# A two-block transformer kernel: latent heads scored in pairs, and the HGRN block's RMS root moved behind its projections

## The reference, cut to what matters

```python
x = layer_norm(DN_ALPHA * x + gate * y, ln_g[layer, 1], ln_b[layer, 1])   # the last line of the first block

def rmsnorm(x, gain):
    y = xf * lax.rsqrt(jnp.mean(xf * xf, axis=-1, keepdims=True) + EPS)
    return (y * gain).astype(x.dtype)

h = h + hgrn2_mixer(rmsnorm(h, hgrn_norm[l]), w_q, w_f, w_i, w_g, ...)
    q = silu(xn @ w_q);  forget = lb + (1 - lb) * sigmoid(xn @ w_f)
    v = xn @ w_i;        gate = silu(xn @ w_g)
```

```python
s = einsum('bqhd,bkhd->bhqk', qn, k_nope) + einsum('bqhr,bkr->bhqk', qr, k_rope)
s = where(k_pos <= q_pos, s * scale, -inf);  p = softmax(s);  o = einsum('bhqk,bkhv->bqhv', p, v)
```

## Time and profile before

| | |
|---|---|
| median of 3 runs | 1435.94 us (1432.33 to 1441.17) |
| the profiled execution | 1434.05 us, its span 1432.3 us |
| TensorE busy | 1340.0 us, 94% of the span |
| VectorE busy | 1006.3 us, 70% |
| ScalarE busy | 593.3 us, 41% |
| chain that ended last | TensorE 80%, VectorE 10%, DMA 4%, ScalarE 3%, issue 2% |
| mean granted clock of TensorE | 0.967 |

### The profile page before, as it was taken

The page is one execution under the profiler, slowest core; times in us unless marked ns, Lnnn a source line. Parts: engine busy times, 40 slices in busy tenths (PEclk is TensorE's granted clock), DMA queues, the critical chain, the costliest instruction groups (busy, mean ns, idle before and its releaser), DMA issues.

```text
span 1432.3 us, 20744 instructions
## 1 busy us (share of the span) xinstructions
PE 1340.0 (94%) x7946; PEld 1127.5 (79%) x7946; DVE 1006.3 (70%) x1345; ACT 593.3 (41%) x796; POOL 13.3 (1%) x23
## 2 busy tenths in 40 slices
PE   5986989999999989999979989999999999999997
PEld 1763678888798878888869987888888777888886
DVE  2767488988878778867776785766668565566665
ACT  2443443434344543343354323543437543543432
POOL 0000000000000000000000000000000000000000
PEclk7997989999999989999989999999999999999999
DMA  9753428878377436656535330555553330455540
GB/s 381 285 199 118 165 101 323 332 268 307 122 261 243 148 118 250 249 209 220 187 120 198 118 118 30 207 193 188 180 201 118 118 118 30 162 210 201 194 158 30
DMA packets 45791, 264.18 MB, mean 184 GB/s; under 512 B 5399, under 2 KB 7063, under 8 KB 19994
## 3 DMA queue, kind: packets, MB, share of 16 engines
q1 hardware_dynamic: 32624, 218.19, 41.8%
q10 hardware_dynamic: 13102, 45.09, 9.1%
HBM read 260.89 MB, written 1.05 MB: 183 GB/s over the span
## 4 chain that ended last, share of the span: by engine, by line
PE 80%; DVE 10%; DMA 4%; ACT 3%; issue 2%; SPq 0%; POOL 0%; DVEq 0%; ACTq 0%; POOLq 0%
PE banks L555 16%; PE banks L557 15%; PE banks L556 15%; PE banks L878 14%; PE banks L881 7%; DMA A<-ada_w 2%; PE banks L834 2%; PE banks L1177 2%; DVE w_lo L1781 2%; PE banks L774 1%; DMA raw<-stream 1%; PE banks L721 1%; ACT w_hi L1219 1%; PE banks L756 1%; PE banks L787 1%
## 5 line engine op out<-in xcount | busy, mean ns | idle before, releaser
L1781 DVE TENSOR_TENSOR w_lo<-raw,w_hi 128x2048 fp32r<-128x2048 f32 x193 | 439.5, 2287 | 122.0 <-ACT w_hi L1219 119.8
L1219 ACT ACTIVATE w_hi<-raw 128x2048 fp32r<-128x2048 f32 x193 | 368.3, 1914 | 226.7 <-PE banks L557 199.5
L878 PE MATMUL banks<-hT,w_hi 128*128 128x512 f32 x896 | 280.8, 395 | 0.0
L555 PE MATMUL banks<-w_hi,R 128*128 128x512 f32 (+1 forms) x624 | 245.0, 393 | 6.4 <-DVE R L1761 3.4
L556 PE MATMUL banks<-w_lo,R 128*128 128x512 f32 (+1 forms) x624 | 242.0, 388 | 0.0
L557 PE MATMUL banks<-w_hi,R 128*128 128x512 f32 (+1 forms) x624 | 242.0, 388 | 0.0
L881 PEld LDWEIGHTS banks<-hT,w_lo 128*128 128x128 f32 x896 | 168.3, 188 | 39.2
L881 PE MATMUL banks<-hT,w_lo 128*128 128x256 f32 x896 | 176.0, 278 | 0.0
L555 PE MATMUL banks<-hT,w_hi 128*128 128x256 f32 x536 | 159.1, 297 | 7.9 <-DVE hT L2240 5.6
L556 PE MATMUL banks<-hT,w_hi 128*128 128x256 f32 x536 | 154.6, 288 | 0.0
L557 PE MATMUL banks<-hT,w_lo 128*128 128x256 f32 x536 | 154.5, 288 | 0.0
(11 more groups left out here) (254 smaller groups left out, 1515.9 us busy)
## 6 DMA issues: line engine op xcount, KB each, us to landing
raw<-stream SPq DMA_DIRECT2D x193, 1024.0 KB, 4.8
A<-ada_w ACTq DMA_DIRECT2D x73, 512.0 KB, 5.5
A<-ada_w SPq DMA_DIRECT2D x6, 1024.0 KB, 16.7
raw<-ada_w SPq DMA_DIRECT2D x3, 1024.0 KB, 7.4
A<-ln_g ACTq DMA_DIRECT2D x4, 512.0 KB, 3.8
A<-ln_b ACTq DMA_DIRECT2D x4, 512.0 KB, 5.6
...
```

The costliest lines, as they stand in the source:

```text
L555: pe.matmul(o, lh, rh, start=start, stop=False, skip_group_check=True)
L878: pe.matmul(two(B[2 * kp + a]), wh[:, kt, P * a:P * a + P], hT[:, :, kt, :], start=kt == 0, stop=False, skip_group_check=True)
L1219: act.activation(w_hi[:, s, :], raw[:, s, :], ACT.Copy).then_inc(hi_done, 1)
L1781: v.tensor_tensor(w_lo[:, s, :], raw[:, s, :], w_hi[:, s, :], ALU.subtract).then_inc(lo_done, 1)
```

## The change

Two edits are joined. At the seam, `hT` is now made from the layer norm's result before its own gain: the columns `sc_c` and `bi_c` hold the layer norm's gain and bias, each times the RMS gain, so `hT` is the input of the projections but for one factor per token, the RMS root. That factor is worked out afterwards from the squares (GpSimd's `root(2, 2, ...)`), and is applied to the projections' results: by ScalarE as the scale of its read for value and gate fills (half the root in `nw` for the gate), and for query and forget fills, whose tokens lie along the row, by a multiplication on VectorE with a row that TensorE spreads over the partitions (`token_spread`) and ScalarE copies out of bank 2 (`token_row`). The two led value fills go to banks 4 and 5. `hg_start` stands behind the two value fills, and VectorE's finishing of a query or forget fill is a step of its own, `bend`, behind the next `rest`.

In latent attention `qk_pair(k)` scores heads k and k+1 at every even step: first the four 128-row products, then the four 64-row products, the two heads' in turn (head k's rows are partitions 0 to 63, head k+1's are 64 to 127), then one mask matmul per head over both blocks. The pairs take banks 4, 5 and 2, 3 in turn, VectorE takes both heads' maxima at the even step, and the transposes behind steps 11 to 17 use banks 0 and 1.

```diff
+        def fill_bank(u, i):
+            return {HG: 4, HG + 1: 5}.get(u, i % 2)
...
-            value = lambda u, j: fills(u, "N", "h", "plain", [arena(H_V, TT, D)[:, :, 256 * j:256 * j + 256]])
-            s = [("hg_start",)] + value(HG, 0) + rest(HG + 4) + value(HG + 1, 1) + rest(HG + 5)
+            value = lambda u, j: fills(u, "N", "h", "value", [arena(H_V, TT, D)[:, :, 256 * j:256 * j + 256]])
+            s = value(HG, 0) + rest(HG + 4) + value(HG + 1, 1) + [("hg_start",), ("token_row",)]
             for j in range(4):
-                s += fills(HG + 2 + j, "T", "h", "silu", [A[:, H_Q + 512 * j:H_Q + 512 * (j + 1)]]) + rest(HG + 6 + j)
+                f = fills(HG + 2 + j, "T", "h", "silu", [A[:, H_Q + 512 * j:H_Q + 512 * (j + 1)]])
+                s += f + rest(HG + 5 + j) + [("bend",) + f[0][1:]]
                 if j == 1:
                     s += [("clear",)]
             for j in range(4):
-                s += fills(HG + 6 + j, "T", "h", "forget", [j]) + rest(HG + 10 + j)
+                f = fills(HG + 6 + j, "T", "h", "forget", [j])
+                s += f + rest(HG + 9 + j) + [("bend",) + f[0][1:]]
+            s += rest(HG + 13)
...
-        STEPS += bound(3, "lnrms", M1 + 31, own("hgrn"), lead=(HG, HG + 1)) + hg_steps()
+        STEPS += bound(3, "lnrms", M1 + 31, mod, lead=(HG, HG + 1)) + hg_steps()
...
+                if reader in ("silu", "forget"):
+                    n["z"] += 1
+                    held[b] = (z_done, n["z"])
+                if u == HG + 2:
+                    pe.wait_ge(token_root, 1)
+                    claim(2)
+                    pe.matmul(B[2][:, 0:256], ones[:, :], A[:, H_DIAG:H_DIAG + 256], start=True, stop=True).then_inc(token_spread, 1)
+                    held[2] = (token_row, 1)
...
-            def qk(k):
-                h, bank = head(k), B[4 + k % 2]
-                all_of(h["units"])
-                if k >= 2:
-                    pe.wait_ge(exp_done, k - 1)
+            def qk_pair(k):
+                heads = [head(k), head(k + 1)]
+                at = 4 if k % 4 == 0 else 2
+                for h in heads:
+                    all_of(h["units"])
+                if at == 2:
+                    for b in (2, 3):
+                        claim(b)
+                        held[b] = (exp_done, k + b - 1)
+                elif k >= 4:
+                    pe.wait_ge(exp_done, k - 2)
+                part = lambda e, t: B[at + e][:, 0:128] if t == 0 else B[at + e][:, 128:384]
+                for e in range(2):
+                    for t in range(TT):
+                        q, kk, _, _ = heads[e]["qk"][0]
+                        pe.matmul(part(e, t), q[:, P * t:P * t + P], kk[:, 0:P * (t + 1)], start=t == 0, stop=False,
+                                  skip_group_check=True)
                 for t in range(TT):
-                    o = bank[:, 0:128] if t == 0 else bank[:, 128:384]
-                    for i, (q, kk, off, w) in enumerate(h["qk"]):
-                        pe.matmul(o, q[off:off + w, P * t:P * t + P], kk[off:off + w, 0:P * (t + 1)], start=i == 0,
+                    for e in range(2):
+                        q, kk, off, w = heads[e]["qk"][1]
+                        pe.matmul(part(e, t), q[off:off + w, P * t:P * t + P], kk[off:off + w, 0:P * (t + 1)], start=False,
                                   stop=False, skip_group_check=True)
-                    m = pe.matmul(bank[:, 256 * t:256 * t + P], ident_b[:, :], causal_b[:, :], start=False, stop=True,
-                                  skip_group_check=True)
-                m.then_inc(s_done, 1)
+                for e in range(2):
+                    pe.matmul(B[at + e].rearrange("p (a b) -> p a b", b=256)[:, :, 0:P], ident_b[:, :],
+                              causal_b[:, :].unsqueeze(1).to_broadcast([P, 2, P]), start=False, stop=True,
+                              skip_group_check=True).then_inc(s_done, 1)
...
-                        if reader == "silu":
-                            act.activation(dst, bank[:, :], ACT.Copy, scale=0.5)
-                        elif reader == "gate":
-                            act.activation(dst, two(bank[:, :]), ACT.Copy, scale=0.5)
-                        act.activation(e, bank[:, :], ACT.Tanh, scale=0.5).then_inc(e_done, 1)
+                        if reader == "gate":
+                            for t in range(TT):
+                                y = bank[:, 256 * t:256 * t + 256]
+                                act.activation(dst[:, t, :], y, ACT.Identity, scale=nw[:, 0, t:t + 1], bias=zero8[:, 0:1])
+                                ins = act.activation(e[:, 256 * t:256 * t + 256], y, ACT.Tanh, scale=nw[:, 0, t:t + 1])
+                        else:
+                            act.wait_ge(z_done, n["e"] + 1)
+                            ins = act.activation(e, dst if reader == "silu" else e, ACT.Tanh)
+                        ins.then_inc(e_done, 1)
...
                     if what == "lnrms":
                         normalise(0, False)
-                        square(0)
-                        normalise(0, True)
-                        normalise(1, False)
+                        act.wait_ge(col_ready, b + 2)
                         turned(0, 0, *scales)
                         turned(1, 1, *scales)
-                        square(1)
                         ahead(last_unit - 1)
-                        normalise(1, True)
+                        normalise(1, False)
                         n["pair"] += 1
                         turned(3, 3, *scales)
                         ahead(last_unit)
+                        square(0)
+                        square(1)
...
+                elif kind == "token_row":
+                    act.wait_ge(token_spread, 1)
+                    act.activation(A[:, H_SCALE:H_SCALE + 256], B[2][:, 0:256], ACT.Copy).then_inc(token_row, 1)
...
+                    if reader in ("silu", "forget"):
+                        z = dst if reader == "silu" else A[:, H_E + 512 * (n["z"] % 2):][:, 0:512]
+                        n["z"] += 1
+                        v.wait_ge(unit_done, u + 1)
+                        v.wait_ge(token_row, 1)
+                        v.tensor_tensor(two(z), two(B[fill_bank(u, n["fill"])][:, :]),
+                                        A[:, H_SCALE:H_SCALE + 256].unsqueeze(1).to_broadcast([P, 2, SEQ]), ALU.mult).then_inc(z_done, 1)
+                    n["fill"] += 1
+                    if reader == "gate":
+                        bend(reader, dst)
...
                     if what == "lnrms":
+                        g_c, b_c = (vec[:, COL[c] + 3 * KT:COL[c] + 4 * KT] for c in ("ln_g", "ln_b"))
+                        gain = vec[:, COL["hgrn"]:COL["hgrn"] + KT]
+                        mark(v.tensor_tensor(sc_c[:, :], g_c, gain, ALU.mult))
+                        v.tensor_tensor(bi_c[:, :], b_c, gain, ALU.mult).then_inc(col_ready, 1)
                         residual(0)
                         row_root(0, False)
-                        residual(1, (0,))
+                        residual(1)
+                        split_part(0, 0)
+                        row_variance(1, False)
+                        split_part(0, 1)
+                        row_shift(1)
+                        half(False)
                         normalised()
                         affine(0)
-                        residual(1, (1,))
-                        square_root(0)
-                        row_root(1, False)
-                        half(False)
+                        stage()
+                        low(last_unit + SLOTS - 1, (last_unit - 1) % SLOTS)
                         v.wait_ge(half_ready, n["half"])
-                        n["n"] += 1
                         normalised()
                         affine(1)
-                        split_tile(0, hT_hi, hT_lo)
-                        square_root(1)
-                        half(True)
-                        stage()
+                        low(last_unit + SLOTS, last_unit % SLOTS)
+                        for t in range(TT):
+                            n["sq"] += 1
+                            v.wait_ge(sq_done, n["sq"])
+                        link(v.tensor_tensor(ve[:, 2:4], ss[:, :, 0], ss[:, :, 1], ALU.add))
+                        v.tensor_scalar(ve[:, 2:4], ve[:, 2:4], 1.0 / D, RMS_EPS, ALU.mult, ALU.add).then_inc(var_ready, 1)
+                        root_made()
+                        link(v.tensor_scalar(nw[:, 0, 0:2], rstd[:, 2:4], 0.5, None, ALU.mult))
+                        for t in range(TT):
+                            ins = v.tensor_scalar(A[:, H_DIAG + P * t:][:, 0:P], ident[:, :], nw[:, 0, t:t + 1], None, ALU.mult)
+                        ins.then_inc(token_root, 1)
+                        continue
```

116 lines of the change are left out of this document (65 added, 51 removed).

## The result

| | before | joined |
|---|---|---|
| median | 1435.60 us (1432.33 to 1441.17, 4 runs) | 1421.38 us (1420.31 to 1425.12, 4 runs) |
| ratio of the two, 95% interval | | 0.9895 (0.9865 to 0.9924) |
| profiled execution, its span | 1434.05, 1432.3 | 1425.12, 1423.3 |
| TensorE busy | 1340.0 | 1327.8 |
| VectorE busy | 1006.3 | 1009.4 |

The change saves 14.2 us, 10.9 to 19.4 by the interval. The forecast was 1425, 10.5 less than the median of before; the measured time lies in its range, though not in the 1423 to 1427 of its likeliest case. The profiled execution of the joined kernel took 1425.12, the slowest of its four; that this equals the forecast is chance, since it lost its time where nothing was changed: MLP 1's last product ends 3.96 us later than in the profile of before (719.77 for 715.81). In later executions of these kernels that moment lay anywhere from 711.6 to 721.0.

The account below looks back on a forecast made before the run. TensorE, under way for 94% of the span, was taken as the bound. Seam and front 2.8 plus heads 7.7 gave 10.5 us off the median of 1435.94, so 1425 us, range 1417 to 1433.

Parts of the forecast that it names:

- likeliest case: Whole kernel: the forecast itself, 1423 to 1427 us, chance 0.46.
- The seam, what goes: Behind MLP 1: second normalisation, ScalarE's second pass and gain multiplication leave the path; first fill at 719.9, 8.2 us earlier.
- The path to the root: VectorE's work after the first fill up to the RMS root and diagonal blocks: root there at 738.0.
- The stand in front of HG+4: TensorE waits 3.2 us from 746.0, as the level table lands at 745.5; the clock's fall costs 1.9 more.
- no second stand: Rival at the seam: table lands before VectorE is free, or clock stays up; 1420 to 1423 us, chance 0.20.
- The multiplications at nothing: Query and forget fills: eight VectorE multiplications, 5.5 us, cost nothing else, covered by that engine's waits for ScalarE.
- the gate reads at 0.45: Gate fills: four ScalarE instructions of 256 columns for two of 512 cost 0.45 us, once, at the last gate slab.
- Seam and front together: From MLP 1's end through the fills: 2.8 us gained, from -1 to +8.
- The heads: Latent attention with paired scores: 5.9 with fills, 1.0 without, 0.8 at the end; 7.7 us gained, from 4 to 10.
- a pair without fills: Later latent heads: the pair takes 5.9 us where two heads took 6.16, held by the copy that empties bank 6.
- the rule of the Trainium skill: Tiling speeds up TensorE, not PSUM's emptying; by it alone heads with fills gain no more than without, 3 us in all.
- The sum: Whole kernel: 2.8 + 7.7 = 10.5 us off, 1425 us against the median of before.

Follow-up runs that it names:

- table_late: Joined kernel with ScalarE's queue waiting for the second high part (HG+5's) before it issues the level table's load; 1432.41 us, ratio to before 0.9970.
- z_narrow: Joined kernel with the multiplications by the row of roots taking 2 of every 256 columns, same places and waits; 1421.79 us, ratio to before 0.9886.
- gate_whole: Joined kernel with each gate fill read by two ScalarE instructions of 512 columns instead of four of 256; 1421.66 us, ratio to before 0.9893.
- joined_again: The joined kernel unchanged, run once more beside two later kernels; 1421.80 us, ratio to before 0.9899.

## Why the prediction was right, and where it was not

- **The seam, what goes: right.** First fill 8.2 us earlier, measured 8.17; in the frame of before 719.91, forecast 719.9. The clock was low behind it and cost 1.7 for the 1.6 taken.
- **The path to the root: right within 0.6.** VectorE's diagonal blocks end at 741.37, in the frame of before 737.41; forecast 738.0.
- **The stand in front of HG+4: wrong, and the likeliest case with it.** I forecast 3.2 us of waiting and 1.9 for the clock, and got 0.30 and none. The step that failed is "ScalarE, which waits for it, reads HG, makes a high part and reads HG+1, and can issue the table's load while the next high part runs: 742.0". It had the wrong thing hold the load back: the work listed ahead of it, where it was the waits listed ahead of it. In that frame the load went out at 737.89, 4.1 earlier. Its own semaphore had been there for 9.2 us; ScalarE's queue stood at the first read's wait for the root, and once that had ended (741.40) it issued the load within 0.45 us, with the first of the six instructions running and five not begun. The load took 4.9 us to land and not 3.5, which ate 1.4 of the 4.1, and the multiplication ended at 746.23 instead of 749.2. table_late forces the load behind the work, as I had taken it, and gives the stand (6.40) and the fall of the clock; the rival "no second stand", with a chance of 0.20 and 1420 to 1423, was what happened. It was a near thing: the table landed (746.75) 0.1 us behind the moment at which VectorE was free (746.63), and neither had slack.
- **The multiplications at nothing, the gate reads at 0.45: right** (z_narrow under 0.4, gate_whole 0.44 to 0.59).
- **Seam and front together: 2.8 forecast, 5.2 to 6.9 measured.** HG+4 started 8.1 us earlier (754.4 - 715.81 = 38.6 before, by the earlier trace rows, and 750.25 - 719.77 = 30.5) where the forecast had 5.2 for the start and 3.3 with the clock's loss behind it. So the forecast was 4.8 too low at HG+4 (2.9 of standing, 1.9 of clock). Behind it, it charged 0.45 and the traces lost 2.9 (8.1 to 5.2), or 1.2 without the clock's fall in the last scan level, which was not in the forecast. That the total for seam and front missed by 2.4 in the joined profile, and not by 4.8, is luck: one error covered part of the other.
- **The heads: right, 7.73 for 7.7.** With fills, first score to head 8's: 1158.18 - 1123.91 = 34.27 for 40.22 before, 5.95 (forecast 5.9). Behind them 32.14 for 33.92, 1.78 (forecast 1.8). Scores of a pair 2.5 for 2.56, a pair without fills 5.91 for 5.9, ended by the copy that empties bank 6, as forecast. So the rule of the Trainium skill (TensorEngine Tiling (Array Packing), section "PSUM Bottleneck") fits the heads without fills, where only 1.8 us came, and not those with fills, where the emptying lay beside TensorE's other work. The rule speaks of a fourfold speed-up; here the 64-row products became 2.4 times as fast (2.10 to 0.86).
- **The sum.** By the traces 12.9 us (5.17 + 7.73) to 14.7 (6.95 + 7.73); by the times 14.2, and 15.2 for joined_again (its before had 1436.96), for a forecast of 10.5.
